# Pre-split tiles for the second down projection, a rewritten end, and new orders of start, gate and transfers in a one-core decoder layer

## The reference

```python
mod = (silu(c) @ ada_w + ada_b)                  # 6 rows of 1024: sh1 sc1 g1 sh2 sc2 g2
h = rmsnorm(x, norm1_g) * (1 + sc1) + sh1
proj = h @ w_in                                  # columns: z 1024, xbc 1536, dt 16, u and v 2048
xbc = silu(causal_dwconv4(xbc)); y = ssd_chunked(xs, softplus(dt), a, bm, cm) + d * xs
y = rmsnorm_groups(y * silu(z)) * ssd_norm_g
g_out = rmsnorm(gelu(u) * (tril(ws) @ rmsnorm(gelu(v)) + bs)) * gm_out_g
x = x + g1 * (concat(y, g_out) @ w_out)
h = rmsnorm(x, norm2_g) * (1 + sc2) + sh2
gate, val = split(h @ ff_up)                     # 2 x 2816 columns
x = x + g2 * ((silu(causal_dwconv3(gate)) * val) @ ff_down)
out = rmsnorm(x, final_g)
```

## Time and profile before

| | |
|---|---|
| median of 3 runs (lowest, highest) | 2851.23 us (2851.18, 2851.54) |
| the profiled execution, its span | 2852.3 us, 2850.4 us |
| PE busy, VectorE, ACT, POOL | 2705.3, 1849.8, 983.9, 1094.9 us |
| mean granted clock | 0.983 |
| mixer 1, first to last unit | 443.95 to 800.00 us |
| mixer 3, first to last unit | 1811.80 to 2152.90 us |
| last down projection | 2597.27 us to 2817.0 us |

### The profile page before, as it was taken

One profiled execution on the slowest core, in us unless ns is written; L12 is line 12 of the kernel. 1 busy time (PEld: TensorE's weight loads), 2 busy tenths in 40 slices (PEclk: granted clock), 3 DMA queues, 4 the chain that ended last, 5 costly groups with the idle time before them and its releaser, 6 DMA issues.

```text
span 2850.4 us, 33659 instructions
## 1 busy us (share of the span) xinstructions
PE 2705.3 (95%) x12363; PEld 2207.4 (77%) x12363; DVE 1849.8 (65%) x2610; ACT 983.9 (35%) x1472; POOL 1094.9 (38%) x736
## 2 busy tenths in 40 slices
PE   3899989899999999999999999999999999999994
PEld 3778868688777888877878888888887888887783
DVE  5777955658467656568786466555737745456868
ACT  2453333322143333344534212233114433334342
POOL 3344431545137777644560000000004544444455
PEclk8899999999999999999999999999999999999997
DMA  9587777999755665573447546665464444437343
GB/s 349 188 299 280 258 266 230 352 350 326 262 183 181 219 210 189 184 280 89 159 153 254 177 156 237 196 221 186 144 225 156 128 126 126 123 110 281 89 131 123
DMA packets 252063, 584.02 MB, mean 205 GB/s; under 512 B 25621, under 2 KB 83449, under 8 KB 247803
## 3 DMA queue, kind: packets, MB, share of 16 engines
q1 hardware_dynamic: 250662, 579.54, 59.9%
q10 hardware_dynamic: 1238, 2.34, 0.2%
HBM read 448.48 MB, written 133.31 MB: 204 GB/s over the span
## 4 chain that ended last, share of the span: by engine, by line
PE 72%; DVE 10%; DMA 7%; POOL 4%; issue 4%; SPq 2%; ACT 1%; DVEq 0%; ACTq 0%; POOLq 0%
PE main L1798 30%; PE pair L2069 14%; PE main L2069 14%; PE main L2083 4%; PE pair L2083 4%; POOL tb L657 2%; DMA t_up_scratch<-tb 2%; DMA tb<-in_ff_up_dram 2%; DVE a_lo L1469 2%; PE pair L1936 1%; DMA w_split_scratch<-w_hl 1%; POOL w_hl L646 1%; DVE mod_sum L1112 1%; SPq L431 1%; SPq L439 1%
## 5 line engine op out<-in xcount | busy, mean ns | idle before, releaser
L646 POOL TENSOR_TENSOR w_hl<-w_raw,w_hl 128x512 fp32r<-128x512 f32 x568 | 828.7, 1463 | 1551.8 <-ACT w_hl L750 1549.5
L750 ACT ACTIVATE w_hl<-w_raw 128x512 fp32r<-128x512 f32 x568 | 355.2, 630 | 867.8 <-PE main L2069 177.8
L1798 PE MATMUL main<-w_hl,h_hi 128*128 128x512 f32 x1536 | 493.6, 403 | 6.3 <-DMA w_hl<-w_split_scratch 5.4
L1798 PEld LDWEIGHTS main<-w_hl,h_hi 128*128 128x128 f32 x1536 | 285.0, 189 | 78.9 <-issue 16.5
L1798 PE MATMUL main<-w_hl,h_lo 128*128 128x512 f32 x768 | 300.9, 392 | 0.0
L657 POOL TENSOR_TENSOR tb<-tb,tb 128x512 f32<-128x512 f32 x132 | 206.2, 1562 | 169.2 <-DMA tb<-in_ff_up_dram 164.5
L1798 PE MATMUL main<-h_hi,w_hl 128*128 128x512 f32 x768 | 250.6, 401 | 11.8 <-POOL h_lo L664 5.4
L1469 DVE TENSOR_TENSOR a_lo<-g,a_hi 128x512 fp32r<-128x512 f32 x132 | 184.1, 1403 | 101.7 <-ACT a_hi L971 101.4
L2083 PE MATMUL main<-w_hl,a_hi 128*128 128x512 f32 x704 | 224.5, 401 | 18.1 <-DVE a_lo L1469 15.4
L2069 PE MATMUL pair<-s_hi,w_hl 128*128 128x512 f32 x736 | 235.7, 393 | 2.4 <-POOL w_hl L646 2.4
L2069 PE MATMUL main<-s_hi,w_hl 128*128 128x512 f32 x672 | 215.5, 394 | 1.9 <-DVE s_lo L1462 1.2
(11 more groups left out here) (268 smaller groups left out, 4908.8 us busy)
## 6 DMA issues: line engine op xcount, KB each, us to landing
w_hl<-w_split_scratch SPq DMA_DIRECT2D x312, 512.0 KB, 3.9
w_split_scratch<-w_hl SPq DMA_DIRECT2D x104, 512.0 KB, 5.8
w_raw<-t_up_scratch SPq DMA_DIRECT2D x176, 256.0 KB, 2.7
w_raw<-in_ff_up_dram SPq DMA_DIRECT2D x132, 256.0 KB, 3.5
w_raw<-t_down_scratch SPq DMA_DIRECT2D x90, 256.0 KB, 2.6
tb<-in_ff_up_dram SPq DMA_DIRECT2D x88, 256.0 KB, 4.6
t_up_scratch<-tb SPq DMA_DIRECT2D x88, 256.0 KB, 5.5
g_scratch<-c_val SPq DMA_DIRECT2D x44, 512.0 KB, 4.0
```

The lines of the kernel that those rows point to most:

```text
L646: nc.gpsimd.tensor_tensor(w_lo[:, g % RING, :], w_raw[:, g % RING, :], w_hi[:, g % RING, :].bitcast(F32), ALU.subtract).then_inc(w_lo_ok, 1)
L750: nc.scalar.activation(w_hi[:, g % RING, :], w_raw[:, g % RING, :], ACT.Copy).then_inc(w_hi_ok, 1)
L1798: ins = T.matmul(main[i], a, w, start=first and p == 0, stop=last and p == 2)
```

## The change

1. *Start.* SP issues the loads of x ahead of ada_w. PE multiplies two of the eight ada tiles directly (`mod_direct`), VectorE adds six; the columns come in two halves; h_lo 0 and 1 go to VectorE, 2 and 3 to POOL; the dt matmuls and their transposes go 3 to 5 units later.
2. *Gate.* The gate matmuls go from (j=1, k=0) to (j=0, k=11) of OUT, norm_x ahead of the gate rows, the x2 loads, gate rows and their store two to four units earlier.
3. *Mixers 1 and 3.* x2 is stored at units 3 to 6 instead of 11 to 14. T_AT[1] goes from every 3.2 units from unit 16 to every 4 from unit 7. The right residual is made in PSUM.
4. *Pre-splits.* 75 of the 77 tiles of FFN 1's down projection are loaded, split and stored in mixer 2 (38, every 1.7 units from unit 22) and mixer 3 (37, every 1.9 from unit 14), through two sets of buffers; the down projection loads the 512 KB split tiles.
5. *Down start.* a_hi and a_lo of the first four tiles come a product earlier, in both FFNs.
6. *End.* Half 1 is finished during P3; the second column half of half 0 is finished bank by bank in PSUM.

```diff
@@ -305,14 +309,22 @@
+        J0 = 2
+        NPRE = ND - J0
+        PRE_AT = {2: [22 + 17 * i // 10 for i in range(38)], 3: [14 + 19 * i // 10 for i in range(NPRE - 38)]}
+        PRE_OF = {2: range(38), 3: range(38, NPRE)}
+        pre_hi_ok = sem("pre_hi_ok")
...
-        T_AT = ((), [16 + 16 * i // 5 for i in range(20)], [18 + 19 * i // 2 for i in range(13)])
+        T_AT = ((), [7 + 4 * i for i in range(20)], [18 + 19 * i // 2 for i in range(13)])
...
+        T_IN = [len([t for t in range(T_OF[2][-1] + 1) if t_set(t) == m]) for m in range(2)]
+        T_ADDS = 4 * (T_OF[2][-1] + 1)
@@ -384,11 +399,13 @@
-                    sp.wait_ge(ada_summed, i - ADA_RING + 1)
+                    sp.wait_ge(mod_col, 1)
...
+            for t in range(NT):
+                sp.dma_start(xn01[:, t, :] if t < 2 else xn23[:, t - 2, :], x[0, t * P:(t + 1) * P, :]).then_inc(x_in, 16)
@@ -445,12 +462,35 @@
...
+            def pre_load(i):
+                p, k = (J0 + i) // KG, (J0 + i) % KG
+                sp.wait_ge(t_st[i % 2], 64 * T_IN[i % 2] + 16 * (i // 2))
+                sp.dma_start(pre_raw[i % 2][:], down_source(p, k)).then_inc(t_ld[i % 2], 16)
+            def pre_store(i):
+                sp.wait_ge(t_add, T_ADDS + i + 1)
+                sp.dma_start(pre_d[i], pre_hl[i % 2][:].bitcast(F32)).then_inc(t_st[i % 2], 16)
...
-                if b % 2 and 11 <= n < 11 + NT:
-                    store_x2(b - 1, n - 11)
+                if b >= 2:
+                    for i, at in zip(PRE_OF[b], PRE_AT[b]):
+                        if n == at + 3:
+                            pre_store(i)
+                    for i, at in zip(PRE_OF[b], PRE_AT[b]):
+                        if n == at:
...
+                            pre_load(i)
+                if b % 2 and 3 <= n < 3 + NT:
+                    store_x2(b - 1, n - 3)
@@ -468,16 +508,16 @@
-                x2_at_unit = OUT + (17 if b else 21)
+                x2_at_unit = OUT + 17
...
-                if b == 0 and n == OUT + 14:
+                if b == 0 and n == OUT + 12:
...
-                if b == 0 and n == OUT + 24:
+                if b == 0 and n == OUT + 20:
@@ -612,8 +654,14 @@
-                    load(f0 + DOWN + j, down_source(p, k))
-                load(f0 + DOWN + ND, td_d[0, 0])
+                    g = f0 + DOWN + j
+                    if loaded(g):
+                        sp.wait_ge(w_used, g + 1)
+                        sp.dma_start(w_hl[:, g % RING, :, :].bitcast(F32), pre_d[j - J0]).then_inc(hl_in[g % RING], 16)
+                    else:
+                        load(g, down_source(p, k))
+                if s + 1 < NSB:
+                    load(f0 + DOWN + ND, td_d[0, 0])
@@ -682,9 +730,14 @@
-                for t in range(NT):
+                for t in range(2):
...
+            def pre_low(i):
+                pool.wait_ge(pre_hi_ok, i + 1)
+                nc.gpsimd.tensor_tensor(pre_hl[i % 2][:, 1, :], pre_raw[i % 2][:], pre_hl[i % 2][:, 0, :].bitcast(F32),
+                                        ALU.subtract).then_inc(t_add, 1)
@@ -694,6 +747,9 @@
+                if b == NB:
+                    for i in range(NPRE):
+                        pre_low(i)
@@ -701,7 +757,7 @@
-                    for j in range(ND + 1):
+                    for j in range(ND + 1 if s + 1 < NSB else J0):
@@ -762,8 +818,17 @@
+            pre_next = [0]
+            def pre_high(b, n):
+                while b >= 2 and pre_next[0] in PRE_OF[b] and PRE_AT[b][pre_next[0] - PRE_OF[b][0]] + 1 <= n:
+                    i = pre_next[0]
+                    pre_next[0] += 1
+                    act.wait_ge(t_ld[i % 2], 64 * T_IN[i % 2] + 16 * (i // 2 + 1))
+                    nc.scalar.activation(pre_hl[i % 2][:, 0, :], pre_raw[i % 2][:], ACT.Copy).then_inc(pre_hi_ok, 1)
...
-                for t in range(NT):
+                for t in range(2):
@@ -998,15 +1066,18 @@
-                    if n == NUP - 1:
+                    if n == NUP - 2:
...
+                    if n == NUP - 1:
+                        a_high(2)
+                        a_high(3)
...
-                    if j + 2 < ND:
+                    if 4 <= j + 2 < ND:
@@ -1129,39 +1200,48 @@
-                ada_sum(i)
...
+            for i in range(ADA_PE, KD):
...
+            for half in range(2):
+                mod_columns(0, slice(4 * half, 4 * half + 4), (main[3 - 2 * half], main[2]), R_N1, 1 + half)
...
+            h_lows(0, (0, 1), aux, full_at)
@@ -1416,11 +1498,22 @@
-                    for t in range(0 if b % 2 else NT):
+                    if b % 2:
+                        for t in range(NT):
...
+                            link(V.tensor_tensor(main[t], main[t], g_bc[:, W:D], ALU.mult))
+                            V.tensor_tensor(x2[:, t, W:D], x2[:, t, W:D], main[t], ALU.add).then_inc(evacuated, 1)
+                            full(G_OUT + 1, t)
+                            link(V.bn_stats(stats2[:, t, 1, :], x2[:, t, W:D]))
+                            V.bn_aggr(mv[:, t, :], stats2[:, t, :, :]).then_inc(stage_used, 1)
+                        dve.wait_ge(stage_used, (b + 1) * STAGED + 4)
+                        return
+                    for t in range(NT):
...
-                        if b % 2:
-                            take(t)
@@ -1429,19 +1522,18 @@
+                if b % 2 == 0:
+                    norm_x(b + 1, [xnew[:, t, :] for t in range(NT)])
+                if b == 0:
...
-                if b % 2 == 0:
-                    norm_x(b + 1, [xnew[:, t, :] for t in range(NT)])
-                if b == 0:
-                    h_lows(1, range(4), aux, [acc[:, 0, :], acc[:, 1, :]])
...
-                    h_lows(b + 1, range(0 if b else 4, KD), aux, [acc[:, 0, :], acc[:, 1, :]])
+                    h_lows(b + 1, range(KD), aux, [acc[:, 0, :], acc[:, 1, :]])
@@ -1646,25 +1740,32 @@
-                    if (p, k) == (P3, 7):
+                    last_s = s == NSB - 1
+                    if (p, k) == (P3, 5 if last_s else 7):
...
-                    if p == P3 and 8 <= k < 10:
-                        half_stats(1, 0, 2 * (k - 8))
-                        half_stats(1, 0, 2 * (k - 8) + 1)
+                    at = 6 if last_s else 8
+                    if p == P3 and at <= k < at + 2:
+                        half_stats(1, 0, 2 * (k - at))
+                        half_stats(1, 0, 2 * (k - at) + 1)
+                    if last_s and (p, k) == (P3, 7):
+                        dve.wait_ge(pool_fin, s * 6 + 6)
+                        add_y(s, 1, 1)
+                    if last_s and (p, k) == (P3, 8):
+                        for t in range(NT):
+                            last = half_stats(1, 1, t)
+                        link(last)
+                    if last_s and (p, k) == (P3, 9):
+                        for t in range(NT):
+                            link(V.bn_aggr(mv[:, 4 + t, :], fstats[:, 1, t, :, :]))
+                        rms_rstd(NT, r1_ok, 4)
...
-                    finish1(s)
...
+                    dve.wait_ge(pool_fin, s * 6 + 8)
+                    c12, xx = y_half[0][:, :, W:D], x_half[0][:, :, W:D]
+                    V.tensor_tensor(xx, xx, c12, ALU.add).then_inc(y0_free, 1)
+                    dve.wait_ge(r1_ok, 1)
+                    dve.wait_ge(fg_in, 16 * (s + 1))
+                    finish_scale(1, y20_ok, (2, 3))
@@ -1709,28 +1810,28 @@
...
-                    take_p3(s, t)
-                    c12, xx = y_half[0][:, t, W:D], x_half[0][:, t, W:D]
-                    dve.wait_ge(d_add, s * (12 + NT) + 12 + t + 1)
...
+                    xx = x_half[0][:, t, W:D]
+                    link(V.tensor_tensor(main[t], main[t], g2_bc[:, W:D], ALU.mult))
+                    V.tensor_tensor(xx, xx, main[t], ALU.add).then_inc(y0_free, 1)
+                    dve.wait_ge(y0_free, 2 + t + 1)
+                    link(half_stats(0, 1, t))
+                    last = V.bn_aggr(mv[:, t, :], fstats[:, 0, t, :, :])
+                link(last)
...
-                dve.wait_ge(fg_in, 16 * (s + 1))
@@ -1764,21 +1862,37 @@
-            def mod_column(n, bank):
...
+            def mod_column(n, ks, bank):
...
+                for k in ks:
...
+                        last = T.matmul(bank[:, m:m + 1], mod_sum[:, 2 * n + part, k * P:(k + 1) * P], ones,
...
+            def mod_direct(bank):
...
+                for k in range(ADA_PE):
+                    pe.wait_ge(ada_in[k], 16)
...
-                    last = T.matmul(bank[:, m:m + 1], mod_sum[:, 2 * n + m // KD, (m % KD) * P:(m % KD + 1) * P], ones,
...
+                    for k in range(ADA_PE):
+                        T.matmul(bank[:, m:m + 1], ada_t[:, (k + ADA_FIRST) % ADA_RING, m * P:(m + 1) * P], c_act[:, k:k + 1],
+                                 start=k == 0, stop=k == ADA_PE - 1)
...
+            mod_direct(main[2])
...
-            pe.wait_ge(ada_summed, KD)
-            mod_column(0, main[3])
+            pe.wait_ge(ada_summed, KD - ADA_PE)
```

(11 more changed lines are left out.)

178 lines of the change are left out of this document (98 added, 80 removed).

## The result

| | before | changed |
|---|---|---|
| median of runs | 2851.2 us | 2925.0 us |
| lowest, highest | 2847.8, 2851.5 | 2919.3, 2926.9 |
| span of the profiled execution | 2850.4 | 2925.0 |

The changed kernel is slower: ratio 1.0258, 95% interval 1.024 to 1.0276, +74 us. Slower was forecast as the likelier sign, at 2864; the time lies 35 us above the stated range.

The account below looks back on a forecast made before the run. TensorE, busy 2705.3 of 2850.4 us, was taken as the bound. Terms -9 -11.9 +9.5 +23.7 -2.9 +11 +4.5 +5.7 -19.5 +1.5 summed to +12.6, giving 2864 us; the range ran from 2820 to 2890.

Parts of the forecast that it names:

- the term of the pre-splits: Mixers 2 and 3: each tile blocks SP 6.2 us, 5.2 of it landing; +11 in mixer 2, +4.5 in mixer 3.
- Rival 3: Pre-split stores land in 5.8 us, making mixer 2 +33 and mixer 3 +13, 2894 us in all; chance 0.13.
- have room: Mixers 2 and 3: ACT and POOL can take the splits, being busy 94 and 3 of mixer 3's 341 us.
- T tiles: Mixer 1: stores, loads, landing and add form a serial circuit in SP's queue, taken at 15.8 us; +23.7.
- Unit 3: Mixers 1 and 3: its weight load stands behind x2's store, which waits for xn2; +9.5 and +5.7.
- Gate: Mixer 0's OUT: the 9.19 us gap and 2.7 us of slow clock behind it go; -11.9.
- First unit: Start: x loaded first and ada tiles shared with TensorE bring it from 57.27 to 46.8 us; -10.5.
- give-back: Mixer 0's first eight units crawl while VectorE adds the second group of ada tiles; 1.5 us returned.
- The last down projection: FFN 1: ready-split tiles keep ACT and POOL out of the way of a_hi and a_lo; -8.5.
- The tail: After the last matmul: half 1 already finished, banks taken in PSUM; 22.4 us instead of 33.4, -11.
- sharing of SBUF interfaces: Mixers 2 and 3: each POOL subtract could hold VectorE back by 2 us; not in the sum, 15 if a tenth exposed.
- Slow clock: After two new stalls of over 5 us PE runs below full clock for some us; +1.5.

Follow-up runs that it names:

- experiment 5: Changed kernel, two output buffers kept; SyncE's load waits only for GpSimd's subtract, GpSimd makes hi and lo and waits for the store's landing: 2845.9 us.
- experiment 6: Changed kernel, two output buffers kept; SyncE's load waits only for GpSimd's subtract, ScalarE makes hi and waits for the store's landing: 2844.4 us.
- experiment 2: Changed kernel with the hi part of each pre-split made by GpSimd instead of ScalarE: 2912.5 us.
- experiment 4: Changed kernel with three output buffers, loads waiting for GpSimd's subtract instead of a landing, and hi on GpSimd: 2843.3 us.
- experiment 7: Kernel of experiment 3 with mixer 1's old table of T tiles, every 3.2 units from unit 16: 2832.6 us, mixer 1 372.9.
- experiment 9: Kernel of experiment 3 with each T tile stored six units after its load instead of four: 2823.4 us, mixer 1 369.0.
- experiment 8: Kernel of experiment 7 with x2 in mixer 1 stored at units 11 to 14 again: 2822.2 us, mixer 1 364.6.
- experiment 10: Kernel of experiment 3 with the gate part of mixer 0 undone: 2849.1 us, mixer 0 387.9 against 382.9.
- experiment 1: Changed kernel with 3 pre-splits instead of 75, POOL doing only the last four final steps, after the last low: 2850.6 us.
- experiment 3: Changed kernel with three output buffers instead of two, each load waiting for GpSimd's subtract instead of a store's landing: 2844.5 us.

## Why the prediction was wrong

**What failed** is the term of the pre-splits: "each tile blocks SP from the issue of a store to its landing: 5.2 us for 512 KB beside weight loads". The blocking was right and is shown by experiments 5 and 6. The landing was mis-sized. 5.2 is the row of four x2 stores in a mixer without pre-splits; the pre-split stores landed in 6.5. The kernel before already had such a row, in the very mixer to which the pre-splits were added (its window 1470 to 1800 us, stores of finished output):

```profile
out_dram<-x_half SPq DMA_DIRECT2D x8, 512.0 KB, 6.5
```

With 6.5 the prediction's own sum gives 6.5 + 0.4 + 0.6 = 7.5 us per tile against 6.1, 6.2 and 5.0 us of PE: 19 x 1.4 + 9 x 1.3 + 8 x 2.5 = 58, where 59.0 was measured, and the raw loads came 7.58 us apart. That it fits to 1 us is partly luck: by the trace SyncE waits 5.7 us per tile (204.6/36), since it may still issue a weight load while the store is landing, and the other 1.9 are issues, some of transfers that the sum doesn't name. The forecast's 11 was small only because 6.2 happened to lie at PE's own pace; above it each tenth of a microsecond counts up to 36 times. Rival 3 named this slope (5.8 us, +33) and got 0.13; it was on the right side and still too short.

In mixer 3 the same working with its landing of 5.8 gives 6.9 us per tile and +13, as rival 3 had it, and 21.2 was measured. The difference of 8 us is not settled: its clock fell to 0.98, gaps of 8.6 us in all end on ScalarE's operations, and with hi on GpSimd it is 2 to 5 us shorter (experiments 2, 4 and 5).

**ACT and POOL "have room"** was true as busy time and looked past their streams: a wait for a load stood there 188 us. Experiment 2 shows that it was worth about 4 us in each mixer. Experiment 6 shows that it costs nothing in mixer 2 once the loads are on time; in mixer 3 about 3 us stay. Of the two causes that the waits view gives half each in mixer 2, one was mostly passing on the other's delay.

**T tiles.** The circuit was right in kind: 15.4 us measured, 15.3 in the earlier trace rows, 15.8 taken. At 15.3 the prediction's sum was 33 - 4 - 15 = +14; experiment 7 gives 13.7. Taking 15.8 "near the undisturbed circuit" added 10 us that weren't there. Two readings of the earlier trace rows were wrong beside that: SyncE did have work in the 7.7 us, and the circuit wasn't undisturbed, since SyncE issued three weight loads and, at 678.30, the loads of the other set. Experiment 9 bears out the rule of the Trainium skill that the prediction weighed here (DMA: Bandwidth & Descriptors, Rules for kernel authors: issue early, wait late): with the wait two units later mixer 1 took 17.6 us less.

**Unit 3.** +9.5 and +5.7 forecast; gaps of 9.05 and 5.78. Experiment 8 got back 8.3.

**Gate.** -11.9 forecast, -5.6 in the traces and about -5 by experiment 10. I counted a gap and the slow clock behind it as gone and did not ask what would be late next on VectorE.

**Start and end.** First unit -10.5 forecast, -10.1 measured; in the experiments, whose start is the same, it comes at 43.0 to 46.7, so the fit to 0.4 is in part luck. The give-back in mixer 0 before OUT was 7.5 instead of 1.5 in this profile and 0.4 to 9.7 in the others, with the same code; why it spreads so is open. The last down projection, -8.5 forecast and -11.0 measured, is right by errors that cancel: by experiment 1 the pre-splits bring 15 and the other changes cost 4. Its base was misread too, for the earlier trace rows shows the third unit, not the first: from 2594.4 on there are 900 matmuls, 75 units, and all 77 take 228.3 us. The tail fell by 11.5 (11 forecast). VectorE's timeline of the changed kernel at the end, which answers to the earlier trace rows:

```profile
2896.27 4.45 DVE L1765 TENSOR_TENSOR x_half<-x_half,y_half 128x2048 f32<-128x2048 f32 x1
2900.65 4.61 DVE L1815 SCALAR_TENSOR_TENSOR x_half<-x_half,rstd,fg_bc 128x1024 f32<-128x1024 f32 x2
2905.18 0.68 DVE L1828 TENSOR_TENSOR main<-main,g_bc 128x512 f32<-128x512 f32 x1
...
2907.47 0.67 DVE L1828 TENSOR_TENSOR main<-main,g_bc 128x512 f32<-128x512 f32 x1
```

The x_half add took 4.45 (4.5 was taken), a bank 2.3 from one L1828 to the next, as forecast; the two gains beside GpSimd 2.3 each instead of 1.2. In the mixers the sharing of SBUF interfaces that the other rule speaks of (the Trainium skill, GPSIMD Engine Reference, Key points) cost PE next to nothing: mixer 2 takes 343.1 us with 38 of GpSimd's subtracts (experiment 3) and 341.1 without (experiment 1). VectorE's busy time there is 230.5 us for 215.8 before, 0.4 per subtract instead of the 2 that the prediction allowed.

**Slow clock.** I gave it 1.5. PE's busy time in mixers 1 to 3 grew by 8.1, 18.2 and 9.4 with the same instructions, 36 us in all, beside 77 of added idle time (15.0, 40.8 and 21.5). In mixer 2 this is no term of its own: SyncE sets the pace of 7.58 us per tile, whose sum gives the 59.0 without it, so a slower PE there fills time in which it would have waited. What the clock cost in mixers 1 and 3 no run separates.

## What to carry to other kernels

When one in-order stream issues the loads that feed the bottleneck, no wait for a landing belongs in it; give it to the engine that is the next to touch the buffer. Here that moved 2.7% by the ratios of experiment 6 and the changed kernel, 77 us, with the same transfers, order and buffers.

A term that comes out near zero because two rates nearly agree, and is multiplied by the number of tiles, deserves the widest bounds of the sum. Take the landing from the busiest row of the same kind and size, here 6.5 us, not from that of a quiet stretch.

## What the runs showed that was not expected

A gap of TensorE can be followed by some microseconds at the lower of its two clocks, and can also not be. In mixer 2 of the changed kernel the granted clock was 0.50 for 6 us behind the 3.52 us gap that ends at 1555.95 and for nearly 3 us behind the one of 3.46 that ends at 1651.25; behind the one of 3.39 that ends at 1754.95 it stayed at 1.00. Over the mixer it was 0.96, where the kernel before had 1.00.

With 38 stores beside them the 512 KB weight loads land in 4.9 to 5.1 us instead of 3.5, and PE has no gap from it (343.7 us at 287 GB/s). Four slots of the ring hold four units of 2.72 us, 10.9 us in all, which is more than that; this reason is argued, not tested.
